# Prompt attention in a hybrid DeltaNet and stick-breaking trunk: both heads of a pair scored together on 64-row halves

## The reference: what is computed

```python
def stick_breaking_block(q, k, v, q_pos, k_pos):
    z = jnp.einsum('bqhd,bshd->bhqs', q, k).astype(jnp.float32) * SB_SCALE
    valid = k_pos[None, :] < q_pos[:, None]
    log_keep = jnp.where(valid, jax.nn.log_sigmoid(-z), 0.0)
    log_rest = lax.cumsum(log_keep, axis=3, reverse=True) - log_keep
    a = jnp.where(valid, jnp.exp(jax.nn.log_sigmoid(z) + log_rest), 0.0)
    return jnp.einsum('bhqs,bshd->bqhd', a.astype(v.dtype), v)
```

## Time and profile before

| | |
|---|---|
| median of three runs | 2358.85 us |
| profiled execution, its own time | 2345.45 us |
| its span, first to last instruction | 2343.7 us |
| PE busy | 2118.2 us, 90% |
| PEld busy | 1949.0 us, 83% |
| DVE busy | 927.0 us, 40% |
| ACT busy | 563.0 us, 24% |
| POOL busy | 646.8 us, 28% |
| mean granted TensorE clock | 0.933 |

### The profile page before, as it was taken

How to read it: one execution, slowest core, us unless ns; L and a number is a source line. 1 busy time by engine, 2 the same in 40 slices (tenths; PEclk the granted TensorE clock), 3 DMA queues, 4 the chain that set the end, 5 groups by cost and what they waited for, 6 DMA issues and landing times.

```text
span 2343.7 us, 33718 instructions
## 1 busy us (share of the span) xinstructions
PE 2118.2 (90%) x13913; PEld 1949.0 (83%) x13913; DVE 927.0 (40%) x1188; ACT 563.0 (24%) x926; POOL 646.8 (28%) x308
## 2 busy tenths in 40 slices
PE   5999999677777599999999899999999999999799
PEld 4999899555553488888889799999999999999577
DVE  5540245566762255555554225221212212214422
ACT  4221223344443222223332203010110100102210
POOL 5222223111100522222220034342344343434100
PEclk9999999888888789988888699999999999999899
DMA  5112221100004200000000211111111111111101
GB/s 159 37 57 100 65 73 46 65 0 0 0 0 137 75 15 19 19 18 18 18 8 6 83 37 40 45 49 48 36 54 54 36 53 37 54 36 58 54 34 38
DMA packets 90814, 104.06 MB, mean 44 GB/s; under 512 B 9444, under 2 KB 74288, under 8 KB 90736
## 3 DMA queue, kind: packets, MB, share of 16 engines
q1 hardware_dynamic: 81392, 89.95, 12.1%
q10 hardware_dynamic: 9344, 12.98, 1.5%
HBM read 85.32 MB, written 17.60 MB: 44 GB/s over the span
## 4 chain that ended last, share of the span: by engine, by line
PE 80%; DVE 9%; ACT 5%; issue 3%; POOL 2%; DMA 2%; SPq 0%; ACTq 0%; DVEq 0%; POOLq 0%
PE psum L1552 41%; PE psum L1524 4%; PE psum L1525 4%; PE psum L1526 4%; PE psum L1818 3%; PE psum L1829 3%; PE psum L1833 3%; DVE area L1231 2%; PE psum L1595 2%; PE psum L1750 2%; PE psum L1619 2%; PE psum L1791 1%; PE psum L1789 1%; DVE area L1232 1%; PE psum L1608 1%
## 5 line engine op out<-in xcount | busy, mean ns | idle before, releaser
L663 POOL TENSOR_TENSOR w_hi<-w_raw,ones 128x2048 fp32r<-128x2048 f32 x51 | 184.7, 3622 | 889.4 <-PE psum L1552 627.2
L1552 PE MATMUL psum<-act_hi,w_hi 128*128 128x352 f32 x1248 | 270.6, 325 | 0.5 <-ACT area L1050 0.5
L1552 PE MATMUL psum<-act_hi,w_lo 128*128 128x352 f32 x1248 | 269.4, 323 | 0.0
L1552 PE MATMUL psum<-act_lo,w_hi 128*128 128x352 f32 x1248 | 269.1, 324 | 0.0
L664 POOL TENSOR_TENSOR w_lo<-w_raw,w_hi 128x2048 fp32r<-128x2048 f32 x51 | 255.2, 5004 | 4.0
L1524 PE MATMUL psum<-w_hi,act_hi 128*128 128x256 f32 (+1 forms) x720 | 226.2, 314 | 28.3 <-issue 17.2
L1525 PE MATMUL psum<-w_lo,act_hi 128*128 128x256 f32 (+1 forms) x720 | 221.5, 308 | 0.0
L1526 PE MATMUL psum<-w_hi,act_lo 128*128 128x256 f32 (+1 forms) x720 | 220.7, 307 | 0.0
L1404 DVE TENSOR_TENSOR area<-psum,area 128x1056 f32<-128x1056 f32 x72 | 90.5, 1257 | 320.5 <-PE psum L1552 320.5
L1552 PEld LDWEIGHTS psum<-act_hi,w_lo 128*128 128x128 f32 x1248 | 214.6, 188 | 0.0
L1552 PEld LDWEIGHTS psum<-act_hi,w_hi 128*128 128x128 f32 x1248 | 213.0, 189 | 0.6 <-ACT area L1050 0.6
(11 more groups left out here) (274 smaller groups left out, 3371.3 us busy)
## 6 DMA issues: line engine op xcount, KB each, us to landing
w_raw<-in_w_up_dram SPq DMA_DIRECT2D x16, 1024.0 KB, 5.5
w_raw<-in_w_down_dram SPq DMA_DIRECT2D x16, 1024.0 KB, 5.1
w_raw<-in_w_in_dram SPq DMA_DIRECT2D x14, 1024.0 KB, 5.6
area<-in_x_prompt_dram SPq DMA_DIRECT2D x16, 512.0 KB, 4.2
conv_scratch<-area ACTq DMA_DIRECT2D x12, 512.0 KB, 2.6
area<-conv_scratch SPq DMA_DIRECT2D x8, 768.0 KB, 4.5
w_raw<-in_cache_k_dram SPq DMA_DIRECT2D x2, 2048.0 KB, 8.1
area<-in_cache_v_dram SPq DMA_DIRECT2D x2, 2048.0 KB, 8.0
```

What stands on the lines that cost most here:

```text
L663: own.link(pool.tensor_tensor(hi, w_raw[:, slot, :], ones[:, 0:1].to_broadcast([P, BLK]), ALU.mult))
L1552: last = pe.matmul(bank(base + c)[0:rows, 0:CH], w(k), a[:, k, CH * c:CH * (c + 1)], start=(k == 0 and w is lhs_hi and a is hi), stop=(k = ...
```

## The change

The queries are no longer staged. `scores(i, t)` makes both heads of a tile at once: head 0 uses rows 0 to 63 of queries and keys, head 1 rows 64 to 127, and their calls alternate. `values(i, t)` also does both heads: the values are the weights (128 rows, 64 columns) and 128 columns of transposed attention stream, so the output comes feature-major, head 0 on partitions 0 to 63 and head 1 on 64 to 127. `copy_out` and `turn_out` go, and `split_out` reads the output directly. For tiles of up to 512 keys the transposes of the two heads have a bank each (`turned`), so they need not wait for the other's copy. PE's loop over the passes is written out four times. The order on PE is now transposes 2t, values t-1, scores t+1, transposes 2t+1; on ACT copy j, sigmoids j+2.

```diff
@@ -453,6 +449,13 @@
 
 
             return UNITS * i + max(j - lag + 1, 0)
+
+        def turned(j):
+
+            u, w = j % 2, P * (j // 2 + 1)
+            if w <= 512:
+                return bank(4 + u)[:, 0:w]
+            return psum[:, 4:6, :].rearrange("p b c -> p (b c)")[:, 0:w]
 
         block = ctx.enter_context(nc.Block())
 ...
-            own.link(pool.memset(q_stage, 0.0))
-            with pool.Fori(0, WT) as i:
-                for j in range(UNITS):
-                    u, t = j % 2, j // 2
-                    pool.wait_ge(scores_ready, 1 + earlier(i, j, 2))
-                    pool.wait_ge(q_staged, 1 + UNITS * i + j)
-                    rows = slice(HD * u, HD * (u + 1))
-                    src = q_t[rows, bass.ds(i, 1), P * t:P * (t + 1)].rearrange("p o t -> p (o t)")
-                    pool.tensor_tensor(q_stage[rows, u, :], src, ones[rows, :], ALU.mult).then_inc(q_staged, 1)
-
-
-            pool.wait_ge(q_staged, 1 + UNITS * WT)
 ...
             def sigmoids(i, j):
                 u, w = j % 2, P * (j // 2 + 1)
-                act.wait_ge(scores_ready, 1 + UNITS * i + j + 1)
+                act.wait_ge(scores_ready, 1 + NT * i + j // 2 + 1)
                 act.wait_ge(att_turned, 1 + earlier(i, j, 2))
                 z = psum[:, 2 * u:2 * u + 2, :].rearrange("p b c -> p (b c)")[:, 0:w]
                 act.activation(keep_buf[:, u, 0:w], z, ACT.Sigmoid, scale=-(HD ** -0.5))
                 act.activation(sig_buf[:, u, 0:w], z, ACT.Sigmoid, scale=HD ** -0.5).then_inc(sig_made, 1)
-
-            def copy_out(i, t):
-                act.wait_ge(o_ready, 1 + UNITS * i + 2 * t + 2)
-                act.activation(o_buf[:, t % 2, :], bank(6 + t % 2)[:, 0:P], ACT.Copy).then_inc(o_copied, 1)
 ...
             def copy_weights(i, j):
                 w = P * (j // 2 + 1)
                 act.wait_ge(att_turned, 1 + UNITS * i + j + 1)
-                act.wait_ge(o_ready, 1 + earlier(i, j, 2))
-                act.activation(at_buf[:, j % 2, 0:w], psum[:, 4:6, :].rearrange("p b c -> p (b c)")[:, 0:w],
-                               ACT.Copy).then_inc(att_placed, 1)
+                act.wait_ge(o_ready, 1 + NT * i + j // 2)
+                act.activation(at_buf[:, j % 2, 0:w], turned(j), ACT.Copy).then_inc(att_placed, 1)
 
             with act.Fori(0, WT) as i:
                 sigmoids(i, 0)
                 sigmoids(i, 1)
-                copy_weights(i, 0)
                 for j in range(UNITS):
+                    copy_weights(i, j)
                     if j + 2 < UNITS:
                         sigmoids(i, j + 2)
-                    if j + 1 < UNITS:
-                        copy_weights(i, j + 1)
-                    if j and j % 2 == 0:
-                        copy_out(i, j // 2 - 1)
-                copy_out(i, NT - 1)
 ...
             def split_out(i, t):
-                dve.wait_ge(o_turned, NT * i + t + 1)
-                src = bank(6 + t % 2)[:, P:2 * P].unsqueeze(1)
+                dve.wait_ge(o_ready, 1 + NT * i + t + 1)
+                src = bank(6 + t % 2)[:, 0:P].unsqueeze(1)
 ...
-            def scores(i, j):
-                u, w = j % 2, P * (j // 2 + 1)
-                pe.wait_ge(q_staged, 1 + UNITS * i + j + 1)
-                pe.wait_ge(sig_made, 1 + earlier(i, j, 2))
+            def scores(i, t):
+                w = P * (t + 1)
+                pe.wait_ge(sig_made, 1 + UNITS * i + 2 * t)
                 for c in range(0, w, 512):
                     n = min(512, w - c)
-                    last = pe.matmul(bank(2 * u + c // 512)[:, 0:n], q_stage[:, u, :],
-                                     k_t[:, bass.ds(i, 1), c:c + n].rearrange("p o t -> p (o t)"),
-                                     start=True, stop=True)
+                    for u in range(2):
+                        rows = slice(HD * u, HD * (u + 1))
+                        last = pe.matmul(bank(2 * u + c // 512)[:, 0:n],
+                                         q_t[rows, i, P * t:P * (t + 1)],
+                                         k_t[rows, i, c:c + n],
+                                         start=True, stop=True)
                 last.then_inc(scores_ready, 1)
 
-            def turn_out(i, t):
-                pe.wait_ge(o_copied, NT * i + t + 1)
-                pe.transpose(bank(6 + t % 2)[:, P:2 * P], o_buf[:, t % 2, :], ident[:]).then_inc(o_turned, 1)
-
             def turn_weights(i, j):
+                t = j // 2
                 pe.wait_ge(att_made, UNITS * i + j + 1)
-                pe.wait_ge(att_placed, 1 + UNITS * i + j)
-                for n in range(j // 2 + 1):
-                    last = pe.transpose(bank(4 + n // 4)[:, P * (n % 4):P * (n % 4 + 1)],
-                                        sig_buf[:, j % 2, P * n:P * (n + 1)], ident[:])
+                pe.wait_ge(att_placed, 1 + UNITS * i + (j - 1 if 2 <= j < 8 else j))
+                for n in range(t + 1):
+                    last = pe.transpose(turned(j)[:, P * n:P * (n + 1)], sig_buf[:, j % 2, P * n:P * (n + 1)], ident[:])
                 last.then_inc(att_turned, 1)
 
-            def values(i, j):
-                u, t = j % 2, j // 2
-                pe.wait_ge(att_placed, 1 + UNITS * i + j + 1)
-                if u == 0:
-                    pe.wait_ge(o_split, 1 + NT * i + max(t - 1, 0))
+            def values(i, t):
+                pe.wait_ge(att_placed, 1 + UNITS * i + 2 * t + 2)
+                pe.wait_ge(o_split, 1 + NT * i + max(t - 1, 0))
                 for n in range(t + 1):
-                    v = v_tok[:, n, bass.ds(P * i + HD * u, HD)]
-                    last = pe.matmul(bank(6 + t % 2)[:, HD * u:HD * (u + 1)], at_buf[:, u, P * n:P * (n + 1)], v,
-                                     start=(n == 0), stop=(n == t))
+                    for u in range(2):
+                        last = pe.matmul(bank(6 + t % 2)[HD * u:HD * (u + 1), 0:P],
+                                         v_tok[:, n, P * i + HD * u:P * i + HD * (u + 1)], at_buf[:, u, P * n:P * (n + 1)],
+                                         start=(n == 0), stop=(n == t))
                 last.then_inc(o_ready, 1)
 
-            with pe.Fori(0, WT) as i:
+            for i in range(WT):
                 scores(i, 0)
-                scores(i, 1)
-                turn_weights(i, 0)
-                for j in range(UNITS):
-                    if j + 2 < UNITS:
-                        scores(i, j + 2)
-                    if j + 1 < UNITS:
-                        turn_weights(i, j + 1)
-                    values(i, j)
-                    if j % 2 and j >= 3:
-                        turn_out(i, (j - 3) // 2)
-                turn_out(i, NT - 1)
+                for t in range(NT):
+                    turn_weights(i, 2 * t)
+                    if t:
+                        values(i, t - 1)
+                    if t + 1 < NT:
+                        scores(i, t + 1)
+                    turn_weights(i, 2 * t + 1)
+                values(i, NT - 1)
```

More of the change, by code:

```diff
@@ L194, in trunk_step @@
         tails_stored = sem("tails_stored")
-        q_staged = sem("q_staged")
         scores_ready = sem("scores_ready")
@@ L202, in trunk_step @@
         o_ready = sem("o_ready")
-        o_copied = sem("o_copied")
-        o_turned = sem("o_turned")
         o_split = sem("o_split")
@@ L345, in trunk_step @@
         at_buf = carve(area, tok0 + 2 * SW, 2, TP)
-        q_stage = carve(area, tok0 + 2 * SW + 2 * TP + 5 * P, 2, P)
         o_buf = carve(area, tok0 + 2 * SW + 2 * TP, 2, P)
@@ L599, in _ @@
             own = Chain(pool, pool_own)
-            pool.sem_inc(q_staged, 1)
             pool.memset(param_rows, 0.0).then_inc(consts_made, 1)
```

## The result

The changed kernel takes 2389.84 us (median of 4 runs, 2389.3 to 2390.36) against 2357.89 for the kernel before (4 runs, 2340.81 to 2365.3) on the same chip: a ratio of 1.0166, 95% interval 1.0125 to 1.0207. It is slower. Its profiled execution took 2389.92 us; that of before had 2345.45, so the two traces lie 44.5 us apart where the medians lie 32 apart.

The account below looks back on a forecast made before the run. A ring of waits between PE, VectorE and ACT, no engine full, was taken to set the pace. Four passes of 74.1 plus 1.5 make 298 us against 265.0, +33: 2378 on the profiled execution, 2392 on the median; range 2344 to 2420.

Parts of the forecast that it names:

- The clock: PE from tile 3 on: idle gaps of 3.7 to 5.6 us exceed 3.38 us, so the granted clock falls to 0.50.
- A third of the bursts at 1.00: Gapless PE stretches from tile 3 on, and the end: a third at full clock, lowering a pass from 78.9 to 74.1 us.
- changes of shape: PE switching tile shape between transposes, values and scores: 0.15 us each, two per tile, 2.4 us a pass (3.0 at lower clock).
- The end: End of a pass, from the last two VectorE units to the next sigmoids: 14.4 us at the upper clock, 17.2 at the lower.
- The first pass: First of the four passes: 1.5 us longer than the second, as in the kernel before.
- The order: PE and ACT queues: scores t+1 now come behind values t-1, so sigmoids wait for scores that used to be out long before.
- ring's sum C: From VectorE's end of unit 2t to the start of 2t+2: 1.45+0.75t us at upper clock, 1.98+1.28t at lower.
- Rivals 1 and 2: Rival 2: PE ahead of VectorE, clock 1.00 from the second tile, 58.2 us a pass, 2328 us; chance 0.07.
- rival 1: Attention stage: clock stays as today, 0.50 for tiles 0 to 2 only; 63.8 us a pass, 2351 us; chance 0.25.
- The halves: Scores of both heads on 64-row halves overlap fully: 0.2135(t+1) us a tile for both, against twice that before.
- Rival 3: Scores and values: the halves do not overlap at 128 and 512 columns; 80.3 us a pass, 2417 us; chance 0.10.
- straight code: PE's written-out loop, four times as much code: taken as zero, with up to 2 us a pass in the range.

Follow-up runs that it names:

- E3: The changed kernel plus products that nobody reads, queued where PE idles, no real work removed: 2348.59 us, ratio 0.9976 to before.
- E5: The kernel before with only PE's loop over the four passes written out as straight code: 2358.93 us, ratio 1.0019.
- E8: The changed kernel, meant to get the order of before; its PE and ACT lists came out the same as the changed kernel's: 2389.03 us, ratio 1.0136.
- E4: The changed kernel with head 1's scores also on rows 0 to 63, so the two heads cannot overlap: 2441.38 us, ratio 1.0347.
- E9: The kernel before, own products, staging and copies kept, with PE's scores j+2 ahead of transposes j and ACT's sigmoids j+2 ahead of copy j: 2319.59 us.
- E2: The changed kernel with PE's scores t+1 ahead of transposes 2t and ACT's sigmoids j+2 ahead of copy j: 2321.96 us, ratio 0.9843.
- E10: E2 plus products that nobody reads, in the same places as in E3: 2314.0 us, ratio 0.9796 to before.

## Why the prediction was right, and where not

**The side and the size.** 2392 was forecast, 2389.84 measured. That is closer than the working deserves, and in part luck. The sum was made against the profiled execution: 2345.45+33 = 2378, and that pair of traces gives 2389.9. The stage grew by 41.8, not 33; the remainder of the agreement comes from putting 33 on a median 13 us above that execution. The changed kernel's runs lie within 1.1 us of each other, those of before within 24.5, and no trace here shows where the slower runs of before spend their time. On record is only that the clock goes with it: of 19 further runs of before the fastest (2338.11 us) had a granted clock of 0.936 over the span, the slowest (2373.14) 0.920.

**The clock: right.** Idle gaps of 4.0 to 5.6 us were forecast before the even unit's transposes; 4.23, 4.74 and up to 6.0 were found. The granted clock over a pass, forecast 0.6 to 0.75, was 0.65 to 0.71. A third of the bursts at 1.00 gave 74.1 us a pass; 75.2, 75.1 and 76.1 were measured. E3 shows that this is the cause and not a companion: its second pass for tiles 0 to 4 and the end, its first for tiles 5 and 6. One piece of the argument was too simple: all gaps were held against the one of 3.38 us. In E3 the clock fell behind a gap of 2.06 us in one pass (the row of 537.24) and not in another (474.60), so the length of the gap alone doesn't tell.

**The terms that were mis-sized.** Tiles 0 to 6 of the second pass: forecast 57.4 (58.7, plus 2.6 for changes of shape, less 3.9), measured 56.8. The end: forecast 16.7, measured 18.4, as it ran nearly all at 0.50 and ACT's copy waits for values (up to 6.8 us, the longest wait above) before PE can turn the last unit. The first pass: 75.6 forecast, 80.4 measured. Of those 4.8 us, 1.1 is what every pass was short; the others are 1.9 in its tiles, where the clock was at 0.50 for longest, and the opening: 5.4 us from the first scores to VectorE instead of 2.4, of which the sum had carried over only half. The old first pass has the same opening, but its surplus was just 1.5, as its clock was at 1.00 from early on and saved the rest in the tiles.

**The order: the step that failed.** The prediction said "This decides", and that ACT's sigmoids now wait for scores "which used to be out long before". They did not use to be: E5's rows show scores 2t+2 behind transposes 2t and values 2t-1, as after, and E8 is the same list of instructions. The ring's sum C was right for the new kernel (10.53 measured at t = 5, between 8.6 and 11.8), and it was right for the old one, too, which went unnoticed. Had I summed the old ring from its own order (9.92 us from 543.84, below, to 553.76, t = 6, against 9.74), it would have been plain that at equal clock the change takes nothing off the turns and adds only its changes of shape, and nearly the whole difference is the clock. Rivals 1 and 2 suffered from this: both credited the change with passes shorter than 64.8 by virtue of a new ring. At 0.95 E3 took 64.3, about rival 1's 63.8, but that was not against 64.8 at the same clock: the old kernel at 0.94 takes 61.6.

```profile
543.84 0.29 DVE L1228 TENSOR_TENSOR area<-area,below 128x128 f32<-128x128 f32 x1 [1.50 <-ACT area L904]
```

A sign that spoke against the step stood in its own list of what would show it. ACT's sigmoids were to wait for scores more than 72.6 us; they waited 32.4. The waits became half as many (28 against 56), of about the same length: the other head's scores, which used to come separately, now come along.

**The halves: right.** Full overlap was taken from 64-column rows; 512-column ones overlap as fully (1.99 us against 3.70 in E4, both at 1.00). Rival 3 is out: the time it gave, 2417, was for lost overlap at today's clock, and E4 with a falling clock as well is at 2441. The Trainium skill ("TensorE: Matmul & The Clock Gate", Part 3) states 3.07x for four row tiles, by which 16 us were to be added; two tiles show no such loss here (1.99 us for both heads, against 1.94 for the four full-height records of one head).

**Changes of shape and straight code: right.** At t = 6 the values start 1.68 us after the transposes (568.54 to 570.22), where seven at the lower clock, 0.213 each, are 1.49: 0.19 for the change, forecast 0.15. The two on the ring together show as 0.26 to 0.29 us a turn at the full clock (E3's first pass against E5). E5 puts straight code at nothing.

**Removed copies:** POOL's 64 copies, 32 output copies and 32 transposes brought nothing, as said. E9 keeps them all and is as fast as E2.

## What to carry to other kernels

Before costing a change that makes an engine's work shorter, write out its queue before and after, and mark which instructions lie on the ring between two waits. Work that lies beside the ring is worth nothing, and on TensorE it can be worth less than nothing: here it kept the clock up, and a stage with 18 us less of PE's busy time became 42 longer. Where a ring of three engines sets the pace, the first thing to try is the order (what is queued ahead of the wait): two loops reordered took the old kernel from 2361.6 (its runs beside it) to 2319.6, while the new products gained nothing in either order: they lost 32 us in the old one, and made no measurable difference in the new one.

## What the runs showed of the hardware

- Two fp32 products on the upper and lower 64 rows, 512 columns each, run at the time of one: 1.99 us for eight records, 3.70 on the same rows (E4), both at the full clock.
- Products that nobody reads paid for themselves here: 41 us in E3, and in E10 a clock of 1.00 over the whole of two passes (0.85 without them), 3 us a pass each, and 8 us on the kernel's median (2314.0 against 2322.0, though the intervals of the ratios overlap).
- With PE busy 20.28 of 34.00 us and gaps of 1.81 us at most, the clock stays at 1.00 (E2); with 15.93 of 23.70 and gaps of up to 2.86 it stays at 0.50 (after). The share of busy time doesn't tell them apart: it was higher in the slow stretch, because the half clock itself makes PE busy longer (six transposes take 1.28 us in the after kernel's turn of t = 5, 0.87 in E3's).
- The same gap of 2.06 us ahead of the same burst left the clock at 1.00 in one pass of E3 and was followed by 0.50 in the next.
- What follows the stage varied from 1640 to 1652 us among kernels that differ only inside it. Gains of 10 us read off one stage of one trace are therefore not yet gains of the kernel.
